# The first adaLN modulation computed in four rounds instead of two, with the first tiles' matmuls between the rounds

## The reference, cut to what matters

```
mod = (silu(cond) @ w_mod + b_mod)          # w_mod: 1024 x 9216, cond: two vectors (context, latent)
sh1, sc1, g1, sh2, sc2, g2, sh3, sc3, g3 = split(mod, 9)      # 1024 columns each
h = rms_norm(x, norm_pre[0]) * (1.0 + sc1) + sh1
g, u = split(h @ ffn_w_in[0], 2)            # ffn_w_in[0]: 1024 x 5632
x = x + 0.5 * g1 * rms_norm((silu(g) * u) @ ffn_w_out[0], norm_post[0])
```

## Time and profile before

| | us |
|---|---|
| median of 3 runs | 1401.72 |
| lowest and highest | 1401.58, 1401.97 |
| the profiled execution, its own time | 1401.38 |
| span of the profiled execution | 1399.2 |

### The profile page before, as it was taken

How to read it: one execution, slowest core, us unless ns; L and a number is a source line. 1 busy time by engine, 2 the same in 40 slices (tenths; PEclk the granted TensorE clock), 3 DMA queues, 4 the chain that set the end, 5 groups by cost and what they waited for, 6 DMA issues and landing times.

```text
span 1399.2 us, 23472 instructions
## 1 busy us (share of the span) xinstructions
PE 1376.1 (98%) x9537; PEld 1258.3 (90%) x9537; DVE 745.8 (53%) x1109; ACT 582.2 (42%) x946; POOL 727.0 (52%) x530
## 2 busy tenths in 40 slices
PE   6999999999999999999999999999999999999998
PEld 5789898999887888999999999988999999998886
DVE  5686555766702421478776312135877666676033
ACT  5243333334534663244445222257344443455243
POOL 1475546465966672323223433542576555667663
PEclk9999999999999999999999999999999999999999
DMA  9756676233535651212112222333122223334465
GB/s 346 260 160 217 214 237 210 62 92 90 176 124 166 194 174 49 61 55 62 53 41 66 76 76 76 103 109 91 46 76 81 78 84 91 91 105 152 135 194 181
DMA packets 215294, 173.34 MB, mean 124 GB/s; under 512 B 6472, under 2 KB 175636, under 8 KB 215060
## 3 DMA queue, kind: packets, MB, share of 16 engines
q1 hardware_dynamic: 212448, 170.61, 39.0%
q10 hardware_dynamic: 2740, 1.24, 0.3%
HBM read 168.65 MB, written 3.17 MB: 123 GB/s over the span
## 4 chain that ended last, share of the span: by engine, by line
PE 89%; DVE 4%; DMA 2%; ACT 2%; POOL 2%; issue 1%; SPq 0%; DVEq 0%; ACTq 0%
PE PP L813 33%; PE PP L611 22%; PE PP L630 8%; PE PP L632 8%; PE PP L631 8%; PE PP L669 2%; DMA W_in<-in_ffn_w_in 1%; PE PP L877 1%; PE PP L655 1%; PE PP L1003 1%; POOL W_lo L541 1%; PE PP L1019 1%; POOL T_lo L550 0%; DVE XTOK L1802 0%; PE PP L1073 0%
## 5 line engine op out<-in xcount | busy, mean ns | idle before, releaser
L541 POOL TENSOR_TENSOR W_lo<-W_in,W_hi 128x512 fp32r<-128x512 f32 (+1 forms) x304 | 382.3, 1283 | 443.5 <-ACT W_hi L1211 436.1
L550 POOL TENSOR_TENSOR W_lo<-W_in,W_hi 128x512 fp32r<-128x512 f32 x112 | 176.3, 1587 | 185.1 <-ACT S_hi L1438 182.0
L1211 ACT ACTIVATE W_hi<-W_in 128x1024 fp32r<-128x1024 f32 x143 | 150.9, 1056 | 226.0 <-PE PP L632 115.8
L630 PE MATMUL PP<-W_hi,Mlo 128*128 128x512 f32 x440 | 172.0, 391 | 1.3 <-POOL W_lo L541 0.9
L632 PE MATMUL PP<-W_hi,Mhi 128*128 128x512 f32 x440 | 171.2, 389 | 0.0
L631 PE MATMUL PP<-W_lo,Mlo 128*128 128x512 f32 x440 | 171.2, 389 | 0.0
L611 PE MATMUL PP<-Hhi,W_hi 128*128 128x320 f32 (+2 forms) x608 | 146.6, 316 | 0.0
L813 PE MATMUL PP<-Hhi,W_hi 128*128 128x320 f32 x452 | 141.3, 313 | 1.3 <-POOL W_lo L550 0.9
L611 PE MATMUL PP<-Hlo,W_hi 128*128 128x320 f32 (+2 forms) x608 | 142.3, 309 | 0.0
L611 PE MATMUL PP<-Hhi,W_lo 128*128 128x320 f32 (+2 forms) x608 | 142.3, 309 | 0.0
L813 PE MATMUL PP<-Hhi,W_lo 128*128 128x320 f32 x452 | 139.6, 309 | 0.0
(11 more groups left out here) (297 smaller groups left out, 3002.3 us busy)
## 6 DMA issues: line engine op xcount, KB each, us to landing
W_in<-in_ffn_w_out SPq DMA_DIRECT2D x176, 256.0 KB, 3.2
W_in<-in_ffn_w_in SPq DMA_DIRECT2D x84, 512.0 KB, 4.5
modl<-in_w_mod SPq DMA_DIRECT2D x14, 2048.0 KB, 7.9
W_in<-in_w_in SPq DMA_DIRECT2D x32, 512.0 KB, 3.8
modw<-in_w_mod SPq DMA_DIRECT2D x4, 2048.0 KB, 14.3
HL<-g_rows SPq DMA_DIRECT2D x6, 512.0 KB, 6.2
V_in<-in_w_in SPq DMA_DIRECT2D x10, 256.0 KB, 3.7
O_in<-in_w_out SPq DMA_DIRECT2D x10, 256.0 KB, 5.4
```

The lines of the kernel that those rows point to most:

```text
L541: return nc.gpsimd.tensor_tensor(lo[:, k0:k1, :], full[:, k0:k1, :], hi[:, k0:k1, :].bitcast(fp32), ALU.subtract)
L550: return nc.gpsimd.tensor_tensor(lo, full, hi.bitcast(fp32), ALU.subtract)
L630: mm(out, xh, wh, start=lead and kk == 0, stop=False)
L1211: A(W[i][0], W[i][2], ACT.Copy).then_inc(hi_done, 1)
```

## The change

The two rounds become four (`ROUNDS = 4`), each with 256 columns of shift and of scale, hence two feature tiles. The `modw` tiles are 8 of 128x8x256, loaded in 8 DMAs of 1 MB, in which each contiguous piece in DRAM is 1 KB instead of 2 KB. A round's products use one half of the PSUM bank in turn. Its fold is 2 matmuls instead of 4, its row copy 256 columns instead of 512.

SP loads slabs 0 and 1 after round 0, slab 2 after round 1, then rounds 2 and 3, slab 3 and the first late slab. ACT copies the first row only after the high parts of slabs 0 and 1. DVE makes per round two `MV`, two `Avec`, four `HL` and two `Hlo`. POOL's wait before the first half of slab 2 is for 2 feature tiles instead of 4. `keep_busy` there is 32 instead of 30.

```diff
-MOD_ROUNDS = ((0, 2), (1, 3))
+ROUNDS = 4
+MOD_FIRST = 2 * ROUNDS
...
         load_early_mod(0)
         load_early_mod(1)
-        for n in range(3):
-            load_in0(n)
+        load_in0(0)
+        load_in0(1)
         load_early_mod(2)
         load_early_mod(3)
+        load_in0(2)
+        for i in range(4, 7):
+            load_early_mod(i)
+        load_early_mod(7)
         load_in0(3)
         load_mod(0)
...
-                pool.wait_ge(sem("h0_ready"), (1, KT // 2)[i - 1])
+                pool.wait_ge(sem("h0_ready"), (1, 2)[i - 1])
...
-        fold_mod(0, modrow[0])
+        fold_mod(0, modrow[0], 0)
         pe.wait_ge(sem("x0_feat"), NCH)
-        keep_busy(30, PP[2][:, 1, 0:P])
+        keep_busy(32, PP[2][:, 1, 0:P])
...
-        for k in range(KT // 2):
+        first_slab(0, (0,))
+        first_slab(1, (0,))
+        early_mod(2)
+        early_mod(3)
+        first_slab(0, (1,))
+        fold_mod(1, modrow[1], 64)
+        first_slab(1, (1,))
+        first_slab(2, (0, 1))
+        for k in (2, 3):
             first_slab(0, (k,))
             first_slab(1, (k,))
-        early_mod(2)
-        early_mod(3)
-        first_slab(2, (0,))
-        fold_mod(1, modrow[1])
-        first_slab(2, (1, 2, 3))
-        for n in range(3):
-            first_slab(n, range(KT // 2, KT))
+        early_mod(4)
+        early_mod(5)
+        first_slab(2, (2,))
+        fold_mod(2, modrow[2], 128)
+        first_slab(2, (3,))
+        early_mod(6)
+        early_mod(7)
+        first_slab(0, (4,))
+        fold_mod(3, modrow[3], 192)
+        first_slab(0, (5,))
+        first_slab(1, (4, 5))
+        first_slab(0, (6, 7))
+        first_slab(1, (6, 7))
+        first_slab(2, range(KT // 2, KT))
...
         next_hi()
-        mod_rows(2, modrow[0])
         next_hi()
+        first_rows(0)
         first_hi(0)
         first_hi(1)
         next_hi()
+        first_rows(1)
```

More of the change, by code:

```diff
@@ L225, in hybrid_step_kernel @@
     rowsB = place("rowsB", [36, P], fp32, at=tile_at(8) + 512)
-    modrow = [place(f"modrow{r}", [P, 512], fp32, at=tile_at(8) + 1024 + 2048 * r) for r in range(2)]
+    modrow = [place(f"modrow{r}", [P, 256], fp32, at=tile_at(8) + 1024 + 1024 * r) for r in range(ROUNDS)]
     late_at = [tile_at(MOD_LATE_FREE), tile_at(FT + MOD_LATE_FREE)]
     early_at = late_at[0] + 16384 + 2 * 2048
-    modw = [place(f"modw{s}", [P, KT, 512], fp32, at=at)
-            for s, at in enumerate((h_at + KT * TB, early_at, early_at + 16384, early_at + 2 * 16384))]
+    modw = [place(f"modw{s}", [P, KT, 256], fp32, at=at + s % 2 * 8192) for s, at in enumerate(
+        at for at in (h_at + KT * TB, early_at, early_at + 16384, early_at + 2 * 16384) for _ in range(2))]
     modl = [place(f"modl{s}", [P, KT, 512], fp32, at=late_at[s]) for s in (0, 1)]
@@ L409, in load_early_mod @@
         def load_early_mod(i):
-            n = MOD_ROUNDS[i // 2][i % 2]
-            sp.dma_start(modw[i][:, :, :], wm[:, :, n * 512:(n + 1) * 512]).then_inc(sem(f"modw_in{i}"), 16)
+            first_col = i % 2 * D + i // 2 * 256
+            sp.dma_start(modw[i][:, :, :], wm[:, :, first_col:first_col + 256]).then_inc(sem(f"modw_in{i}"), 16)
         def load(i, k0, kn, src):
@@ L462, in _ @@
         load_early_mod(1)
-        for n in range(3):
-            load_in0(n)
+        load_in0(0)
+        load_in0(1)
         load_early_mod(2)
         load_early_mod(3)
+        load_in0(2)
+        for i in range(4, 7):
+            load_early_mod(i)
+        load_early_mod(7)
         load_in0(3)
         load_mod(0)
-        sp.wait_ge(sem("mod_mm"), MOD_EARLY)
+        sp.wait_ge(sem("mod_mm"), MOD_FIRST)
         load_mod(1)
         def next_mod(i):
-            sp.wait_ge(sem("mod_mm"), MOD_EARLY + (1 if i == 2 else i))
+            sp.wait_ge(sem("mod_mm"), MOD_FIRST + (1 if i == 2 else i))
             load_mod(i)
@@ L480, in _ @@
         load(BASE["in0s"] + 1, 0, KT, w0[:, :, DFF + j * P:DFF + (j + 1) * P])
-        sp.wait_ge(sem("mod_mm"), MOD_EARLY + 2)
+        sp.wait_ge(sem("mod_mm"), MOD_FIRST + 2)
         load(BASE["in0s"], 0, KT, w0[:, :, j * P:(j + 1) * P])
@@ L662, in _, with mod_slab @@
         pe.wait_ge(sem("ones_set"), 2)
-        def mod_slab(w, i, first=False):
+        def mod_slab(w, i, first=False, cols=slice(0, 512)):
             for k in range(KT):
                 q = k % 4
-                m = mm(PP[3][32 * q:32 * q + 32, 0, :], S2[:, k, 30 - 2 * i:62 - 2 * i], w[:, k, :],
+                m = mm(PP[3][32 * q:32 * q + 32, 0, cols], S2[:, k, 30 - 2 * i:62 - 2 * i], w[:, k, :],
                        start=first and k < 4, stop=k >= 4, skip_group_check=not first)
@@ L675, in early_mod, with fold_mod @@
             pe.wait_ge(sem("silu_c"), 2)
[L676 to L680, removed]
+            r = i // 2
+            if r > 1:
+                pe.wait_ge(sem("modrow"), r - 1)
+            mod_slab(modw[i], i % 2, i % 2 == 0, slice(r % 2 * 256, r % 2 * 256 + 256))
+        def fold_mod(i, rows, first_at):
             pe.wait_ge(sem("modrow"), i + 1)
-            for q in range(4):
-                at = i * P + q * 32
+            for q in range(rows.shape[1] // P):
+                at = first_at + q * 32
                 m = mm(PP[3][:, 1, at:at + 32], rows[:, q * P:(q + 1) * P], ident[:, P:P + 32],
@@ L887, in late_mod @@
             if i == 0:
-                pe.wait_ge(sem("modrow"), 2)
+                pe.wait_ge(sem("modrow"), ROUNDS)
             mod_slab(modl[int(i == 1)], i, i == 0)
@@ L927, in _ @@
             if p == last_mod + 1:
-                fold_mod(2, modrowl)
+                fold_mod(ROUNDS, modrowl, 2 * P)
             if p == last_mod + 3:
@@ L1250, in _, with mod_rows, first_rows @@
         A(LB[:, 1:3, :], LB[:, 1:3, :], ACT.Exp).then_inc(sem("lb_exp"), 1)
-        def mod_rows(slabs, rows):
+        def mod_rows(slabs, rows, cols):
             act.wait_ge(sem("mod_mm"), slabs)
-            A(rows[:, :], PP[3][:, 0, :], ACT.Copy).then_inc(sem("modrow"), 1)
+            A(rows[:, :], PP[3][:, 0, cols], ACT.Copy).then_inc(sem("modrow"), 1)
+        def first_rows(r):
+            mod_rows(2 * r + 2, modrow[r], slice(r % 2 * 256, r % 2 * 256 + 256))
         def first_hi(k):
@@ L1265, in _ @@
         next_hi()
+        first_rows(1)
         first_hi(2)
         first_hi(3)
-        mod_rows(MOD_EARLY, modrow[1])
-        for k in range(KT // 2, KT):
-            first_hi(k)
+        first_rows(2)
+        first_hi(4)
+        first_hi(5)
+        first_rows(3)
+        first_hi(6)
+        first_hi(7)
         next_hi()
@@ L1418, in late_rows @@
             if p == last_mod + 1:
-                mod_rows(MOD_EARLY + MOD_LATE, modrowl)
+                mod_rows(MOD_FIRST + MOD_LATE, modrowl, slice(0, 512))
             if p == last_mod + 4:
@@ L1764, in first_affine, with first_vectors, groups @@
             m.then_inc(sem("h0_32"), 1)
+        def first_vectors(r):
+            def groups(ap):
+                step = ap.ap[1][0]
+                return bass.AP(ap.tensor, ap.offset, [ap.ap[0], [KT * step, 2], [step, 2]])
+            span = slice(2 * r, 2 * KT)
+            for cnd in range(2):
+                sums = PP[3][:, 1, 64 * r:64 * r + 64].rearrange("p (q i c) -> p i q c", q=2, c=2)
+                link(V.tensor_tensor(groups(MV[:, span, cnd]), sums[:, 0:2, :, cnd], groups(VA[:, span]), ALU.add))
         dve.wait_ge(sem("x0_feat"), NCH)
-        for r in range(2):
+        for r in range(ROUNDS):
             dve.wait_ge(sem("mod_fold"), r + 1)
-            mod_vectors(r * P, MOD_ROUNDS[r])
-            ks = range(r * KT // 2, (r + 1) * KT // 2)
+            first_vectors(r)
+            ks = range(2 * r, 2 * r + 2)
             gains(0, True, False, ks[0], ks[-1] + 1)
@@ L1974, in late_vectors @@
         def late_vectors():
-            dve.wait_ge(sem("mod_fold"), 3)
+            dve.wait_ge(sem("mod_fold"), ROUNDS + 1)
             mod_vectors(2 * P, range(MOD_EARLY, MOD_EARLY + MOD_LATE))
```

## The result

| | median, us | lowest to highest | runs |
|---|---|---|---|
| before | 1401.57 | 1400.19 to 1402.26 | 9 |
| after | 1405.07 | 1402.52 to 1406.42 | 9 |

The changed kernel is slower: its time is 1.0027 times that of before, 95% interval 1.0019 to 1.0035 (2.7 to 4.9 us); the two medians lie 3.5 us apart. The forecast was 2.0 us with a range up to 1405.4, so the time lies inside the range by 0.3 us. The profiled execution of after happened to be its quickest, 1402.52 us with a span of 1400.3; what is read from it must be held against a second profile, which the first experiment brings.

What follows compares the result with a forecast made beforehand. PE, busy 98% of the span, was taken to bound the kernel. The first late slab 0.3 us later plus 1.7 for the clock made 2.0, so 1401.7 + 2.0 = 1403.7 us, range 1400.2 to 1405.4 (8 in 10).

Steps and rivals of the forecast that it cites:

- collision: POOL's four halves, 29.1 to 34.2 us, run beside DVE's round 1; its two `Avec` wait, delaying tile 2 from 35.3.
- fall of the clock: After PE's 2.3 us gap before tile 2, 3.4 us at half speed on the matmuls of rounds 2 and 3: 1.7 us lost.
- The rate of 1 KB pieces: Modulation loads in 1 KB pieces: 349 GB/s, on the line through 291 for 512 B and 387 for 2 KB.
- Round 0: Loads, row copy, fold and DVE's chain up to the first slab matmul: 25.7 us against 30.5 before, 4.8 us won.
- Slab 1's low half: PE waits for POOL's low half for tile 0 of slab 1, from 26.6 to 27.5 us: 0.9 us idle.
- X: Start of PE's first matmul on tile 2: 36.5 us, the middle taken between 35.9 and 37.1.
- From tile 2 to the late slab: PE's products, modulation slabs and two later chains up to the first late slab: 22.35 us, with two idle gaps of 0.6.
- rival 1: The clock holds through the gap before tile 2, so only 0.3 us stays: 1401.4 to 1402.6 us; chance 0.25.
- The end follows the late slab: The shift of PE's first late slab goes through a load on SP to everything behind it; nothing later catches it up.
- 3, 1 KB like 512 B: Loads in 1 KB pieces move like 512 B ones, late slab 5 us later, 1406.7 us; chance 0.14 with the fourth rival.
- 4, no earlier start: ACT or the transposes hold PE to about 30 us, all three chains added, near the third rival; chance 0.14 with it.
- 2, no collision: DVE gets ahead of POOL or POOL has finished; late slab 1.0 to 1.7 us sooner, 1400.0 to 1400.7 us; chance 0.16.

Runs made afterwards that it cites:

- the first experiment: The changed kernel run again unaltered, with a second profile (span 1402.6 us): median 1405.56 us against 1401.46 for before, ratio 1.0027.
- the kernel with 1 KB pieces: The kernel before with each early modulation slab loaded by two DMAs of 256 columns: 1403.62 us against 1400.89, ratio 1.0021; a second profiled execution took 1405.13.
- the fastest kernel: Changed kernel with POOL's second halves held back, slab 1's low half earlier, rounds 2 and 3's modulation slabs and folds earlier: 1398.94 us against 1400.89, ratio 0.9986.
- the second experiment: The changed kernel with one more POOL wait, holding the three second halves back until four ready tiles: median 1402.22 us, ratio 1.0003.

## Why the prediction was right and where it was wrong

**The kind of outcome** was right: forecast +2.0 us with collision and fall of the clock, measured +3.5 (and +4.1 on the second chip). The mechanism was right; two terms were too small: the delay of the late slab by collision and loads, and the price of the fall. The range held narrowly: 0.3 us from its upper end, and the 4.1 us of the second chip would have put it just outside (both ratios are 1.0027).

**The rate of 1 KB pieces**: 349 GB/s taken, 340 to 350 seen. This window of after, over round 0's loads, answers the earlier trace rows:

```profile
9.70:15.50 5.80, 5.80 (x27) 5.57 (x27) 2.49 (x8) 5.50 (x9) 0.00 (x0) 1.00 1.10 350
```

**Round 0**: first slab matmul forecast at 25.7; seen at 26.64 in after, 25.63 in its second profile, 25.5 to 26.6 in the kernels built on it. The 0.9 us of after's own profile come from the start: its 24 first transposes took 5.38 us, those of the second profile 4.10. Timeline of PE in after, then in the second profile:

```profile
10.12 5.38 PE L660 MATMUL PP<-ident 128*128 128x128 f32 x24
```

```profile
9.97 4.10 PE L660 MATMUL PP<-ident 128*128 128x128 f32 x24
```

From execution to execution PE reaches its full pace at another time, and the forecast had taken one of them for fixed. The expectations speak of a clock that rises late; the granted clock in the rows reads 1.00 all through these stretches, so what the traces show is the pace and not its cause.

**Slab 1's low half**: 0.9 us forecast, 0.66 or 0.67 seen in the first four profiles; right in kind.

**The collision**: `Avec` forecast to wait for two POOL operations, and did. The step that failed is the landing of slab 2 ahead of it: forecast 28.0, seen 29.1, hence POOL from 30.2 to 35.2 instead of 29.1 to 34.2, and X at 37.9 and 37.5 instead of 36.5, outside the bounds given (35.9 to 37.1). Of the 1.0 to 1.4 us that X was late, 0.6 came from taking the middle of the bounds: at the 349 GB/s that were seen the forecast's own steps give 37.1. The rest came from the landing, 1.1 us late, of which the steps behind POOL took some back. The forecast had each load take its bytes by its rate, one behind the other. From slab 1's landing (19.95) to slab 2's (29.10) the queues moved at some 338 GB/s, 3.1 MB in 9.15 us, where round 1 and slab 2 together have 2.6: the loads behind them, issued meanwhile, took their share. That last reading fits the numbers and was not tested by itself. **This term: 0.3 us forecast at the late slab without the clock, 1.6 to 1.9 measured.**

**From tile 2 to the late slab**: 22.35 forecast, 22.53 in after, 22.55 in two experiments. The two later gaps, 0.6 each, were 0.58 and 0.69. This part held to 0.2 us.

**The clock**: the forecast took 1.7 us, the length of the fall before (3.4) halved. The experiments gave 2.66 in the trace and 2.5 in the medians, since the low level lasted until 43 us. The step that was wrong was to take the length of one fall for the length of any. In after's own profile, with a gap of 2.32 us instead of 2.92, it did not fall at all, so rival 1 is a real case of the same kernel. How often it falls I can't say: the nine timed executions of after record mean granted clocks of 0.999 (the profiled one) and 0.998 (the eight others), which fits a fall in most; but on the second chip one at 1.000 took 1405.88.

**The fall in before** was put at nothing in the prediction, since it fell onto transposes without result. The two profiles of the kernel with 1 KB pieces show that it cost something: with the fall the 30 transposes took 5.14 us, as in before, and from the fold to the first slab matmul lay 5.81 us; without it they took 3.47 and 4.57 us lay there, and that matmul waited for DVE. In before it is 5.81 too (24.71 to 30.52). The chain that ended last in before runs over these transposes, from 25.79 on. So some 1.2 us of the time to before's first slab matmul were the clock, in that execution, and part of the 3.9 us won there was not won by the change.

**The end follows the late slab**: right. From it to the first matmul of the next part lie 29.87 us before, 29.82 after, 29.89 in the second profile of after, 29.80 in the fastest kernel. From there to the end of the span the twelve profiles lie between 1310.0 and 1312.3 (before 1310.8) with no relation to the edits that I can see; that alone makes single executions differ by 2 us. The medians did not follow the late slab everywhere: on the second chip the two agree to about 0.5 us, but where the late slab came 1.5 and 3.5 us sooner the medians moved by +0.3 and -2.0. Why is not shown.

**Sum anew**: 1.6 for collision and loads + 2.5 for the clock = 4.1. Both are differences of medians, so that sum must come out; read from the traces alone it is 1.7 + 2.66 = 4.3, against 62.68 - 58.49 = 4.2 seen at the late slab. The change's idea was sound, 3.9 us won at the first matmul; what ate it was one wait of POOL, set to the second tile, the low half of slab 1, and folds placed behind the products that could have covered them. With all three put right it beats before by 2.0 and 2.6 us.

**Rivals.** 1, the clock holds, happened in single executions. 3, 1 KB like 512 B, and 4, no earlier start, were wrong by the rows above. 2, no collision, was made by hand in the second experiment: 1.3 us faster than before forecast, 0.8 slower measured; tile 2 came at 36.20, not 35.3, because that execution's first slab matmul came at 26.58, not 25.7; the 9.6 us between the two are as forecast.

## What to carry to other kernels

Before you let an engine start work sooner, look at which small instructions of its neighbour lie on the critical path at that time: POOL operations of 1.25 us made two `Avec` of 0.18 take 0.75 and 1.23. Put what produces the next input (modulation slabs, fold) ahead of the work that can cover its chain; then a collision can cost nothing, as it did here. And price an idle gap of the matmul engine at its own length plus what the clock may take afterwards (here 2.5 us for a gap of 2.9, in some executions only), and with a load order of several sizes, the landing of the one that matters at an upper bound rather than in a strict row.

## What the runs showed of the hardware

- **Avec against MV beside POOL**: with two inputs in SBUF an instruction of 2 columns waits for the whole POOL operation; with one input in PSUM, of 4 columns, 0.36 us for the pair beside POOL as without it. The Trainium skill (GPSIMD Engine Reference, Specifications) says that POOL shares its SBUF interfaces with DVE instructions of two SBUF inputs; the trace agrees in both cases.
- **POOL waits too**: its four halves took 6.36 us beside two `Hlo`, 5.02 beside two `Avec` and 5.05 beside neither.
- **A fall of the clock** had two lengths: 3.4 us in the earlier trace rows, and from some 36.5 to 43.3 us, in a gap that began at 34.5, in the second profile of after. The same kernel had a fall in one profile and none in the other.
- **Full pace at the start** comes at another time each run: in 14.00:15.00 PE did 7 matmuls in after and 12 in its second profile, though the granted clock of both rows reads 1.00:

```profile
14.00:15.00 1.00, 1.00 (x7) 1.00 (x6) 0.00 (x0) 1.00 (x2) 0.00 (x0) 1.00 1.11 351
```

```profile
14.00:15.00 1.00, 1.00 (x12) 1.00 (x10) 0.02 (x1) 1.00 (x2) 0.00 (x0) 1.00 1.10 347
```

- **1 KB pieces** moved at 340 to 350 GB/s, between 291 for 512 B and 387 for 2 KB; the number of DMAs differed as well.
